# A hybrid decoder block with 32 experts on one core: x and memory loaded turned, the row scale put on behind the projection, and one layer of experts loaded in smaller pieces

## What is computed

```python
def rms_norm(x, w):
    y = xf * lax.rsqrt(jnp.mean(xf * xf, axis=-1, keepdims=True) + NORM_EPS)
    return (y * w).astype(x.dtype)

xn = rms_norm(h, attn_norm_w[l])
mem_n = rms_norm(mem, mem_norm_w[l])
p = xn @ w_in                       # 1024 x 3072: 1792 columns for the recurrence, 1280 for the rest
km, vm = jnp.split(mem_n @ w_mem_kv, 2, axis=-1)
merged = merged + jax.nn.sigmoid(xn @ w_gate[bi]) * (branches[bi] @ w_branch[bi])
...
h = x_pad[tok] @ w1[e] + b1[e]      # w1: 32 x 1024 x 2048
return clamped_swiglu(h) @ w2[e] + b2[e]   # w2: 32 x 1024 x 1024
```

## Time and profile before

| | |
|---|---|
| runs, us | 1276.27, 1276.69, 3164.12 |
| median, us | 1276.69 |
| the profiled execution's own time, us | 1278.25 |
| its span, us | 1276.5 |
| PE busy, us (share) | 1209.3 (95%) |
| DVE busy, us (share) | 371.0 (29%) |
| ACT busy, us (share) | 184.0 (14%) |
| moved by DMA | 448.74 MB, mean 352 GB/s |

### The profile page before, as it was taken

One profiled execution on the slowest core, in us unless ns is written; L12 is line 12 of the kernel. 1 busy time (PEld: TensorE's weight loads), 2 busy tenths in 40 slices (PEclk: granted clock), 3 DMA queues, 4 the chain that ended last, 5 costly groups with the idle time before them and its releaser, 6 DMA issues.

```text
span 1276.5 us, 15523 instructions
## 1 busy us (share of the span) xinstructions
PE 1209.3 (95%) x6554; PEld 594.2 (47%) x6554; DVE 371.0 (29%) x634; ACT 184.0 (14%) x355; POOL 0.2 (0%) x4
## 2 busy tenths in 40 slices
PE   8999999999999999999999999989899898989896
PEld 7887777888544343333333333232323233232322
DVE  2058452411133223133222323222231312322223
ACT  2234621300121010110101010010101011000102
POOL 0000000000000000000000000000000000000000
PEclk9999999999999999999999999999999999999999
DMA  9344212597489999999999999999999999999995
GB/s 350 119 156 149 67 35 68 178 391 317 156 301 407 427 429 427 428 427 428 427 427 428 429 430 428 428 428 428 428 431 428 428 427 428 428 429 429 429 426 239
DMA packets 52710, 448.74 MB, mean 352 GB/s; under 512 B 5649, under 2 KB 18065, under 8 KB 27058
## 3 DMA queue, kind: packets, MB, share of 16 engines
q1 hardware_dynamic: 52272, 447.10, 85.1%
q10 hardware_dynamic: 386, 0.92, 0.2%
HBM read 446.96 MB, written 1.05 MB: 351 GB/s over the span
## 4 chain that ended last, share of the span: by engine, by line
PE 70%; DMA 25%; DVE 4%; issue 1%; ACT 0%; SPq 0%; PEldq 0%; DVEq 0%
PE ps L535 67%; DMA ring<-in_w_exp 18%; DMA upper<-in_w_exp 6%; PE ps L1087 1%; DVE ring L1561 1%; DMA xrows<-in_x 0%; PE ps L796 0%; DVE ring L1664 0%; PE ps L1096 0%; DVE upper L1938 0%; DVE upper L1645 0%; DVE ring L1558 0%; PE ps L702 0%; DVE upper L1600 0%; ACT upper L1271 0%
## 5 line engine op out<-in xcount | busy, mean ns | idle before, releaser
L535 PE MATMUL ps<-ring,upper 128*64 128x512 f32 (+4 forms) x2656 | 508.4, 526 | 29.8 <-DMA ring<-in_w_exp 18.9
L535 PE MATMUL ps<-upper 128*64 128x512 f32 (+5 forms) x1844 | 329.3, 461 | 17.0 <-DMA upper<-in_w_exp 11.8
L535 PEld LDWEIGHTS ps<-ring,upper 128*64 128x64 f32 (+2 forms) x2656 | 164.2, 136 | 340.4 <-issue 292.7
L535 PEld LDWEIGHTS ps<-upper 128*64 128x64 f32 (+3 forms) x1844 | 154.0, 154 | 174.0 <-issue 143.8
L535 PE MATMUL ps<-xT,ring 128*128 128x256 f32 x672 | 150.5, 381 | 0.4 <-DVE xT L1522 0.4
L535 PEld LDWEIGHTS ps<-xT,ring 128*128 128x128 f32 x672 | 126.1, 190 | 18.7 <-issue 1.8
L1854 DVE TENSOR_TENSOR xrows<-xrows,ps 128x1024 f32<-128x1024 f32 x30 | 36.5, 1216 | 268.0 <-PE ps L535 250.5
L1833 DVE TENSOR_TENSOR upper<-ps,merged 128x512 f32<-128x512 f32 x32 | 22.1, 692 | 229.9 <-PEq L1059 216.2
L1421 ACT ACTIVATE xT<-upper 128x512 f32<-128x512 f32 x32 | 20.2, 632 | 374.2 <-DVE upper L1836 374.1
L1427 ACT ACTIVATE factors<-ps 64x512 f32<-64x512 f32 x63 | 37.3, 591 | 246.5 <-PEq L1082 245.8
L535 PE MATMUL ps<-factors,cst 128*128 128x512 f32 x128 | 62.9, 615 | 3.8 <-PE ps L535 2.8
(11 more groups left out here) (234 smaller groups left out, 506.5 us busy)
## 6 DMA issues: line engine op xcount, KB each, us to landing
ring<-in_w_exp SPq DMA_DIRECT2D x120, 2048.0 KB, 34.7
upper<-in_w_exp SPq DMA_DIRECT2D x63, 2048.0 KB, 34.4
ring<-in_w_exp SPq DMA_DIRECT2D x13, 1024.0 KB, 8.1
ring<-in_w_gate SPq DMA_DIRECT2D x9, 1024.0 KB, 5.2
ring<-in_w_in SPq DMA_DIRECT2D x8, 896.0 KB, 12.1
ring<-in_w_in SPq DMA_DIRECT2D x8, 640.0 KB, 3.9
ring<-in_w_branch SPq DMA_DIRECT2D x5, 1024.0 KB, 5.1
ring<-in_w_mem_kv SPq DMA_DIRECT2D x4, 1024.0 KB, 4.9
```

What stands on the lines that cost most here:

```text
L535: return pe.matmul(o, l, r, start=start, stop=stop, skip_group_check=True)
```

## The change

Part one, the start of the mixers:

- The host hands in x and the memory a second time, turned (`x_turned`, `mem_turned`: features on partitions). The rows are still loaded, for the sums of squares and for the residual, but later in SP's order.
- `x_turned` is loaded straight into `xT`: two chunks of features and the parameters from ACT's queue, the other six chunks by SP behind the first chunk of `w_in`. DVE puts the feature weights on in place. PE starts the projection with that, so without the row scale.
- The row scale reaches all partitions by a product: DVE makes a diagonal matrix of it (`diagonal`, identity times scale), PE multiplies it with a block of ones (`spread_scale`, once for x after chunk 1, once for the memory after chunk 3), DVE copies the result out.
- DVE, and no longer ACT, takes the seven banks of the recurrence's projection out of PSUM and multiplies by the row scale on the way. For the 1280 other columns and for the gates, DVE multiplies `xT` in place by the scale (`row_scaled`), each chunk once PE has used it.
- The memory is no longer turned by PE; DVE multiplies it in place with weight and scale. The 32 turns of blocks are gone, and so are ACT's eight copies of the memory. `keep_awake` does five products of ones instead of six of zeros.

Part two, the experts: which transfers are of one slot is told by a list, `single`. Beside the second layers of experts 0 and 1 and the last pieces it now holds the first layer of expert 2, so that its 8 MB come as 8 transfers of 1 MB and not as 4 of 2 MB.

```diff
-    odd_before = [16 if s in (1, 3, RING - 3, RING - 1) else 0 for s in range(RING)]
+    single = [*range(2 * CPE - SIDE - 8, 4 * CPE - SIDE - 16), *range(PASS - 6, PASS)]
@@ SP
-            sp.dma_start(xrows[:, 0, :], x[0, 0:P, :]).then_inc(x_loaded[0], 16)
-            sp.dma_start(cst[:, 0:P], consts[:, 0:P]).then_inc(ident_loaded, 16)
-            sp.dma_start(xrows[:, 1, :], x[0, P:T, :]).then_inc(x_loaded[1], 16)
-            sp.dma_start(prm[:], params).then_inc(prm_loaded, 16)
...
+                if n == 0:
+                    sp.dma_start(xT_flat[:, XT_FIRST * T:], x_turned[:, XT_FIRST * T:]).then_inc(xT_full, 16)
+                if n == 1:
+                    for t in range(TT):
+                        sp.dma_start(xrows[:, t, :], x[0, t * P:(t + 1) * P, :]).then_inc(x_loaded[t], 16)
+                    sp.dma_start(cst[:, 0:P], consts[:, 0:P]).then_inc(ident_loaded, 16)
                 if n == 2:
                     sp.dma_start(memrows, mem[0].rearrange("(t p) d -> p t d", p=P)).then_inc(mem_loaded, 16)
                 if n == 3:
+                    sp.dma_start(memT.rearrange("p c t -> p (c t)"), mem_turned).then_inc(mem_loaded, 16)
@@ load_w1
-                for c in range(begin, min(end, KC - aside(opening, r)), 2):
+                for c in range(begin, min(end, KC - aside(opening, r))):
+                    m = w1_at(c, r, opening)
+                    count = 1 if is_single(a, m) else 2
...
+                    free(n + count, very_first)
@@ PE
-            keep_awake(6, 7, zeros)
-            pe.wait_ge(ident_loaded, 16)
-            for t in range(TT):
-                pe.wait_ge(scaled, t + 1)
-                for c in range(KC):
-                    last = pe.transpose(half(0, c)[:, t * P:(t + 1) * P], xscaled[:, t, c * P:(c + 1) * P], ident)
+            keep_awake(5, 7, unit)
+            def spread_scale(k):
+                pe.wait_ge(scaled, TT * (k + 1))
+                if k:
+                    pe.wait_ge(xT_sb, KC + 1)
+                mm(half(7, 0), unit[:, 0:P], scales[:, k, :]).then_inc(row_ps, 1)
             for c in range(KC):
                 w = take("in_rwkv", c)
+                pe.wait_ge(xT_sb, c + 1)
...
+                if c in (1, 3):
+                    spread_scale(c // 2)
@@ low_rank
-                elif c in (5, 6):
-                    pe.wait_ge(kk_clamped, 1)
...
-                        for t in range(TT):
-                            last = pe.transpose(dst[:, t * P:(t + 1) * P], memrows[:, t, k * P:(k + 1) * P], ident)
@@ ACT
+            act.dma_start(xT_flat[:, 0:XT_FIRST * T], x_turned[:, 0:XT_FIRST * T]).then_inc(xT_first, 16)
+            act.dma_start(prm[:], params).then_inc(prm_loaded, 16)
-            act.wait_ge(mem_loaded, 16)
+            act.wait_ge(mem_loaded, 32)
...
-            for b in range(7):
-                act.wait_ge(rwkv_ps, b + 1)
-                act.activation(raw[:, 2 * b:2 * b + 2, 1:T + 1], ps[:, b, :].rearrange("p (c t) -> p c t", c=2), ACT.Copy).then_inc(raw_sb, 1)
@@ DVE
+            for c in range(KC):
+                if c == 0 or c == XT_FIRST:
+                    dve.wait_ge(xT_full if c else xT_first, 16)
+                TS(xT[:, c, :], xT[:, c, :], col("attn", c), None, ALU.mult).then_inc(xT_sb, 1)
+            def row_scaled(c):
+                dve.wait_ge(xT_sb, c + 1)
+                dve.wait_ge(slots_used, min(c + 1, KC - 1))
+                if c == KC - 1:
+                    dve.wait_ge(rwkv_ps, 7)
+                TTn(xT[:, c, :], xT[:, c, :], row_scale[:, 0, :], ALU.mult).then_inc(xT_sb, 1)
...
+            for k in range(KC):
+                STT(memT[:, k, :], memT[:, k, :], col("memn", k), row_scale[:, 1, :], ALU.mult, ALU.mult).then_inc(memT_sb, 1)
+            for c in range(3, KC - 1):
+                row_scaled(c)
+            for b in range(7):
+                dve.wait_ge(rwkv_ps, b + 1)
+                TTn(raw[:, 2 * b:2 * b + 2, 1:T + 1], ps[:, b, :].rearrange("p (c t) -> p c t", c=2),
+                    row_scale[:, 0, :].unsqueeze(1).to_broadcast([P, 2, T]), ALU.mult).then_inc(raw_sb, 1)
```

More of the change, by code:

```diff
@@ L159, in build @@
     per_pass = [PASS // RING + (s < PASS % RING) for s in range(RING)]
-    odd_before = [16 if s in (1, 3, RING - 3, RING - 1) else 0 for s in range(RING)]
+    single = [*range(2 * CPE - SIDE - 8, 4 * CPE - SIDE - 16), *range(PASS - 6, PASS)]
+    alone = [m for m in single if m % 2] + [PASS + 1]
+    odd_per_pass = [sum(m % RING == s for m in alone) for s in range(RING)]
     with ExitStack() as ctx:
@@ L352, in build, with is_single, odd_full @@
         block = ctx.enter_context(nc.Block())
+        def is_single(a, m):
+            return isinstance(a, int) and a * (GROUP * CPE) + m in single
+        def odd_full(q, m):
+            s = m % RING
+            return q * (16 * odd_per_pass[s]) + 16 * (uses[s] + sum(k % RING == s and k <= m for k in alone))
         def place(q, a, m):
-            s = m % RING
-            return s, q * per_pass[s] + a * TURNS + (m // RING + 1), q * PASS + a * (GROUP * CPE) + m
+            s, n = m % RING, q * PASS + a * (GROUP * CPE) + m
+            if m % 2 == 0:
+                return s, (q * per_pass[s] + a * TURNS + (m // RING + 1)) * 16 + 16 * uses[s], n
+            return s, odd_full(q, a * (GROUP * CPE) + m) if is_single(a, m) else None, n
         def aside(opening, r):
@@ L1059, in up, with down @@
                     pe.sem_inc(up_ps, 1)
-            def down(q, a, r, E, whole=4, final=False, between=None, very_first=False, opening=False):
+            def down(q, a, r, E, final=False, between=None, opening=False):
                 pe.wait_ge(actT_sb, E + 1)
@@ L1065, in down @@
                 for i in range(4):
[L1066 to L1070 removed]
+                    s, full, n = place(q, a, w2_at(i, r, opening))
+                    if full is not None:
+                        pe.wait_ge(slot_full[s], full)
                     for cc in range(2):
@@ L1163, in pair @@
                 if last:
[L1164 to L1165 removed]
+                    down(q, a, r, E, False, turns)
+                    down(q, a, r + 1, E + 1, True)
                 else:
@@ L1236, in _ @@
             act.activation(ss[:, 7:8], epsc[:, 0:1], ACT.Exp)
-            for n in range(2):
-                act.wait_ge(memT_ps, n + 1)
-                for i in range(4):
-                    bank = 7 - i // 2 * 2 if n == 0 else 6 + i // 2
-                    act.activation(memT[:, 4 * n + i, :], ps[:, bank, (i % 2) * T:(i % 2 + 1) * T], ACT.Copy,
-                                   scale=col("memn", 4 * n + i)).then_inc(memT_sb, 1)
             act.wait_ge(csum_sb, 1)
@@ L1965 @@
     arrays["in_consts"] = constants()
+    for name in ("x", "mem"):
+        turned = np.asarray(inputs[name])[0].T.reshape(KC, P, -1).transpose(1, 0, 2)
+        arrays[f"in_{name}_turned"] = np.ascontiguousarray(turned.reshape(P, -1))
     args = [nc.dram_tensor(name, a.shape, F32, kind="ExternalInput").ap() for name, a in arrays.items()]
```

119 lines of the change are left out of this document (58 added, 61 removed).

## The result

| | before | after |
|---|---|---|
| median of 15 runs, us | 1276.88 | 1279.36 |
| lowest, us | 1276.04 | 1278.32 |
| highest, us | 3164.12 | 1280.19 |
| the profiled execution: own time, span, us | 1278.25, 1276.5 | 1278.85, 1277.0 |
| PE busy, us | 1209.3 | 1209.0 |

The ratio of after to before is 1.002, with an interval of 1.0012 to 1.0027. So the change costs 1.5 to 3.4 us, and the measured 1279.36 lies 3.8 us above the end of my range. It is within 2%, as said, but the sign is the other one. Before's run of 3164.12 is the only one of its 15 above 1278.04.

The account below looks back on a forecast made before the run. The experts' DMA stream was taken as the bound, so its earlier start and closed gaps count. 4.0 - 0.87 - 0.1 + 1.0 = 4.0 us takes the span from 1276.5 to 1272.5, forecast 1272.7 us, range 1270.8 to 1275.6.

Parts of the forecast that it names:

- What bounds the kernel: Whole kernel: experts are one DMA stream at a fixed rate, so earlier slot release by the mixers and closed gaps count.
- The start of the projection: Start of the mixers: first product at 7.4 us, when the first chunk of `w_in` lands, DVE's weight products done before.
- The gain of the start: Start of the mixers: first product 4.0 us earlier than the profiled 11.38 us, with 3.4 and 5.2 as bounds.
- The bridge to the median: Whole kernel: median 1276.69 lies 0.2 above the span of 1276.5, so span 1272.5 became forecast 1272.7 us.
- its lower end for the forecast: Whole kernel: 1271.3 us, with the start capped at 3.6, single-slot loads worth 1.5, and rounding.
- The clock: Rival at the projection's start: PE's clock not up at 7.4 us, at most 2.7 us lost, 1275.4 us; chance 0.17.
- The spread products: Projection on PE: two added 128x256 products cost 0.43 us each, 0.87 us for both, and neither wait lasts.
- Later chunks: Projection: chunk 4 of `w_in` lands at 32.1 us, PE asks at 32.6 us, so the added turned inputs stay hidden.
- DVE for ACT at the eviction: End of the projection: DVE keeps up with PE, last bank out 0.1 us later; in-place scalings cost nothing.
- the memory's turns: Mixers behind `kk`: 1.7 us less PE work, counted as nothing because PE waits there already; upper bound 1.7 us.
- Single slots: Expert 2's first layer: halves issued 1.8 us earlier close stream gaps, worth 1.0 us, bounds 0 and 1.5.
- each single transfer pays its own latency: Rival at expert 2's loads: four more transfers, unhidden, cost 10 us, giving 1283.7 us; chance 0.02.

Follow-up runs that it names:

- one-row kernel: Changed kernel with parameters and the two first chunks of turned x in one array, loaded by one ACT-queue transfer, and 7 warm-up products: 1274.29 us, 0.998.
- part two alone: The kernel before with only the single slots of expert 2 added (the memory's root shares a semaphore): 1276.27 us, 0.9995 (0.9986 to 1.0004).

## Why the prediction was wrong, step by step

**What bounds the kernel: right.** What the mixers lost or won went through to the end nearly whole, as the table shows, and the stream stood at its rate in all kernels.

**The start of the projection: the failed step, forecast 7.4, measured 9.95 us.** The size of the large transfer was right (7.2). What failed is the sentence that DVE's two weight products "lie in front of that landing". I had summed bytes over both queues, 1.22 MB passed at 6.0 us, and took it to hold for each of the transfers among them. It holds for the sum. A transfer of 40 KB, the last of a second queue, takes turns with the first queue's large packets, and its bytes say nothing of when it ends. Of the 2.5 us it cost 2.0 (parameters at 9.4, turned x at 7.4). The other 0.5 is DVE's: even the turned x landed behind the 7.2 us of `w_in`, and a weight product and its semaphore stand behind each landing (9.44 to 9.95), so the first product would have come at 7.9 us without the parameters. The late start also lengthened the idle time, and with that it cost the clock as well.

**The gain of the start: 4.0 forecast, about 0.1 measured.** Besides the 2.5 us above, 1.3 us were never there: the 11.38 us from which I subtracted was one late execution. The bridge to the median had the same fault. This execution's own time was 1278.25 and the median 1276.69; I set the median beside the span, which made the two look alike, where a span is to be compared with a time less the 1.8 us that lie around it (1278.25 - 1276.5). The range had a slip of its own: its lower end for the forecast, 1271.3, is 0.4 us below what its two terms give.

**The clock: a rival with 0.17, and it came true.** Its mechanism, a clock that is not up when the projection starts, was told rightly and its price rightly bounded (at most 2.7, measured 2.05). Its chance was the fault: I gave it for an idle time of 1.6 us, which held only if the first product came at 7.4. The two risks were not independent, since a late start lengthens the idle time. Seen so, they belonged together in one rival, 1272.7 + 2.5 + 2.05 = 1277.3 us, and it ends on the slow side.

**The spread products: right.** 0.87 forecast, 0.86 measured by doubling them. PE waited for neither: in the timeline of after the first stands at 24.13 us, right behind the 56 records, and the second at 36.65, behind the next 56.

**Later chunks: right.** In after chunk 4 was issued at 11.91 us and took

```profile
ring<-in_w_in SPq DMA_DIRECT2D x1, 896.0 KB, 19.2
```

so it landed at 31.1 us (forecast 32.1), and PE, later than forecast, asked for it only behind the second spread product. From 28 to 85 us PE was busy for 57.00 of 57.00 us in either kernel. In the one-row kernel, which starts at 6.96 us, it is still hidden: it landed at 30.3 us, and PE asked for it at 32.07.

**DVE for ACT at the eviction, and the memory's turns: right.** DVE keeps up with PE, and the cover behind it stayed, 15.07 us of idle time before L1580 where it was 15.51 before L1548. PE's waits behind the reciprocal grew by what the turns gave back. PE and DVE of after, 85 to 122 us:

```profile
89.86 1.29 DVE L1580 TENSOR_SCALAR ring<-ps 128x512 f32<-128x512 f32 x2 [15.07 <-PE ps L554]
...
106.77 1.12 PE L554 MATMUL ps<-ring,upper 128*128 128x512 f32 x2 [1.42 <-ACT upper L1253]
...
110.68 1.16 PE L554 MATMUL ps<-upper 64*128 64x128 f32 x16 [0.84 <-ACT upper L1262]
```

The wait of 1.42 us at 106.77 is new, that of 0.84 at 110.68 answers to the 0.77 at 109.22 of before. From the reciprocal to PE's long piece it is 153.06 us in before and 153.07 in after. So the 1.7 us were worth nothing, as counted.

**Single slots: mis-sized.** Forecast 1.0 us, measured 0.3 by the times and 0.7 by the traces. The loads did go out 1.8 us sooner, as forecast: SP issued them in after at 377.22 and 384.47 us, with the mixers 1.46 us later than in before, where it was 377.57 and 384.82. The gap that I counted was closed in part; I had taken every dip between 384.5 and 392.5 us for a lack of issued transfers. The one from 386 to 388 stays at 326 GB/s with a DMA share of 1.04: the engines were not short of work there. A transfer of ACT's queue (the experts' bias) is under way in it; whether that makes the dip was not tried. The rival that each single transfer pays its own latency, 10 us, is refuted by part two alone: 0.3 us less and not more, in an interval that ends at 0.5 us more.

## What to carry to other kernels

When several transfers stand ahead of the first product, give the small one a place by packets and not by bytes: at the head of the queue, or as part of the same rows as its neighbour. Alone on a second queue beside a large one it took 5.2 us in place of 1.7, which did no harm only because the first product waited longer for something else. When a change makes PE start sooner, make its warm-up reach the latest start that can be expected, and price a late landing together with the clock that it loses. And before subtracting from one profiled execution, compare its own time with the median: this one was 1.6 us above, and the lateness sat exactly in the stretch that the change was to shorten.

## What was not expected of the hardware

- The same transfer of 40 KB took 1.7, 5.0, 5.2 and 8.2 us, by its queue and its place in it.
- 296 KB in one transfer landed at 6.4 us; the same bytes as 256 + 40 KB in two had landed at 7.4 and 9.4.
- The landing of the second half of x moved from 5.7 to 4.5 us between two executions of the same kernel, and with it all that followed.
- In after the clock fell once more, in the middle of the experts' stream. Stretches of the profile of after:

```profile
508.00:512.00 4.00, 3.69 (x14) 1.14 (x12) 3.10 (x7) 0.63 (x1) 0.00 (x0) 1.00 1.03 438
512.40:515.80 3.40, 3.40 (x10) 0.98 (x8) 1.76 (x3) 0.00 (x0) 0.00 (x0) 0.50 1.03 439
```

There PE had hardly been idle. Six other profiles of this study show the same fall, about 500 us behind the rise, that of before run again among them, and six do not. No loss is to be seen from it, since the DMA stream, at 439 GB/s in that stretch, sets the pace; what makes it stays open.
